# A hybrid decoder layer: sigmoids and gelu by hyperbolic tangents, and the convolution from an SBUF tile with carried columns

## The reference, cut to what matters

```python
lx = causal_depthwise_conv(lx, conv_w[i], conv_b[i])
r = sigmoid(gate_a); i = sigmoid(gate_x)
log_a = -LRU_C * r * softplus(-lam)
a = exp(log_a)
mult = sqrt(-expm1(2.0 * log_a))
bterm = mult * i * x
h[t] = a[t] * h[t-1] + bterm[t]
lru = h * gelu(lg)
mix = concatenate([rmsnorm(attn), rmsnorm(lru)])
x = x + mix @ w_out
```

## Time and profile before

| | us |
|---|---|
| median of 3 runs | 1447.66 |
| all three | 1447.93, 1447.66, 1443.44 |
| the profiled execution, its own time | 1447.09 |
| its span, slowest core (4) | 1445.4 |
| spans of the eight cores | 1414.2 to 1445.4 |
| mean granted TensorE clock, by core | 0.850 to 0.867 |

### The profile page before, as it was taken

How to read it: one execution, slowest core, us unless ns; L and a number is a source line. 1 busy time by engine, 2 the same in 40 slices (tenths; PEclk the granted TensorE clock), 3 DMA queues, 4 the chain that set the end, 5 groups by cost and what they waited for, 6 DMA issues and landing times.

```text
span 1445.4 us, 24745 instructions; the slowest of 8 cores (1414.2 to 1445.4 us)
## 1 busy us (share of the span) xinstructions
PE 1092.8 (76%) x7740; PEld 722.3 (50%) x7834; DVE 698.8 (48%) x1253; ACT 742.1 (51%) x1392; POOL 483.6 (33%) x576
## 2 busy tenths in 40 slices
PE   2535759988979897267697979988988797681892
PEld 1312225555555555156475757766766575550440
DVE  4879995977777864541121212211212121225853
ACT  4778897887877974012232423333333242224882
POOL 3212132332323333024242434433444243220663
PEclk9766777988978978559799989999999899895896
DMA  8999996963705932408999999999989989888422
GB/s 230 193 190 109 107 109 85 189 115 96 132 9 88 144 106 94 184 21 160 204 195 220 175 216 208 204 187 205 234 190 184 223 156 174 174 276 319 163 117 117
DMA packets 69775, 234.93 MB, mean 163 GB/s; under 512 B 23430, under 2 KB 30342, under 8 KB 51472
## 3 DMA queue, kind: packets, MB, share of 16 engines
q0 software_dynamic: 43984, 134.60, 57.1%
q1 hardware_dynamic: 25664, 98.75, 20.1%
HBM read 415.47 MB, written 101.71 MB: 358 GB/s over the span
## 4 chain that ended last, share of the span: by engine, by line
PE 44%; DMA 20%; issue 11%; DVE 9%; ACT 9%; POOL 4%; SPq 1%; another core or an unknown queue 0%; DVEq 0%; ACTq 0%; POOLq 0%
PE ps L1369 13%; DMA sb_R<-h2scr,sb_R 12%; PE ps L1341 7%; PE ps L967 4%; DMA sb_R<-wall,sb_R 3%; DMA sb_R<-w_pg 3%; PE ps L751 3%; PE ps L1324 2%; PE ps L1004 2%; PE ps L1512 2%; PE ps L841 2%; PE ps L903 1%; DMA sb_R<-xin 1%; PE ps L904 1%; PE ps L1245 1%
## 5 line engine op out<-in xcount | busy, mean ns | idle before, releaser
L1369 PE MATMUL ps<-sb_R 128*128 128x256 bf16 x3008 | 343.0, 275 | 5.3 <-DMA sb_R<-wall,sb_R 3.6
L1369 PEld LDWEIGHTS ps<-sb_R 128*128 128x128 bf16 x3008 | 296.0, 99 | 53.3 <-issue 6.7
L1351 POOL DMA_INDIRECT yscr<-sb_R x94 | 94.6, 1006 | 361.1 <-DVE sb_R L1348 344.9
L1374 DVE TENSOR_TENSOR sb_R<-sb_R,ps 128x512 bf16<-128x512 f32 x94 | 64.7, 688 | 296.9 <-PE ps L1369 268.8
L1327 ACT COPY sb_R<-ps 128x1024 bf16<-128x1024 bf16 x94 | 95.1, 1012 | 191.6 <-PE ps L1324 187.3
L1341 PE MATMUL ps<-sb_R 128*128 128x512 bf16 x706 | 171.2, 396 | 4.9 <-issue 2.1
L1348 DVE COPY sb_R<-ps 128x512 f32<-128x512 f32 x94 | 65.0, 692 | 222.5 <-PE ps L1341 140.2
L1373 ACT ACTIVATE sb_R<-ps 128x512 f32<-128x512 f32 x94 | 56.1, 597 | 224.8 <-PE ps L1369 224.7
L1295 POOL DMA_INDIRECT sb_R<-h2scr,sb_R x94 | 97.7, 1039 | 89.3 <-DVE sb_R L1254 60.9
L1341 PEld LDWEIGHTS ps<-sb_R 128*128 128x128 bf16 x752 | 74.5, 102 | 89.0 <-issue 19.8
L1324 PE MATMUL ps<-sb_id,sb_R 128*128 128x128 bf16 x752 | 58.1, 237 | 63.6 <-DMA sb_R<-h2scr,sb_R 63.1
(11 more groups left out here) (234 smaller groups left out, 2085.6 us busy)
## 6 DMA issues: line engine op xcount, KB each, us to landing
sb_R<-wall POOLq DMA_DIRECT2D x66, 1024.0 KB, 23.1
wbf<-wall POOLq DMA_DIRECT2D x30, 1024.0 KB, 46.0
sb_R<-wbf SPq DMA_DIRECT2D x30, 1024.0 KB, 13.2
sb_R<-xin SPq DMA_DIRECT2D x32, 512.0 KB, 20.3
sb_R<-yscr SPq DMA_DIRECT2D x16, 1024.0 KB, 8.1
xscr<-sb_R SPq DMA_DIRECT2D x16, 512.0 KB, 4.1
sb_R<-xscr SPq DMA_DIRECT2D x16, 512.0 KB, 13.4
out<-sb_R SPq DMA_DIRECT2D x16, 512.0 KB, 2.7
```

Of the source, the lines that this page charges most:

```text
L1351: return e.indirect_dma_start(y_d, bass.IndirectOffsetOnAxis(ap=didx[:, blk:blk + 1], axis=0), y.ap, None, bounds_check=breg(e, 2 * T_OWN ...
L1369: ins = e.matmul(pv[:, q * N:(q + 1) * N], lhsT=w_[:, c, f * P:(f + 1) * P], rhs=hT_[:, c, 0:N], start=(c == 0), stop=(c == 7))
L1374: S.op("dve", lambda e: e.tensor_tensor(hid[s % 2][:, fp * 2:fp * 2 + 2, 0:N], sgs[fp][:, 0:2 * N].rearrange("p (q t) -> p q t", q=2), pu. ...
```

## The change

Both sigmoids become 0.5 (1 + tanh(x/2)). One ACT pass makes each tanh; the halves go into the columns of constants (`der` 0 to 3) and into a bias of ln 0.5, so the decay is one Exp from the tanh and the two Ln and the Exp that inverted are gone. 1 + tanh is multiplied with the convolution by one DVE pass, which takes the place of the subtraction. The gelu has one tanh in the place of Exp, Ln, Exp; its factor of a half goes into the norm. The projection is copied by ACT from PSUM to an SBUF tile `lx` of 515 columns, whose first three POOL fills from `carry`; the four DVE passes read shifted pieces of it over the full 512 columns, and POOL saves the last three. There are two such tiles (`LX`), and `F5` shrinks from 12 to 10; `F10` stays at 14. The scheduler learns which functions share a table and ranks an ACT operation that needs another table 20 us lower.

```diff
+SWITCH = 20.0
+SETS = {AF.Exp: ("exp", "ln"), AF.Ln: ("ln",), AF.Tanh: ("exp",), AF.Silu: ("silu",), AF.Sigmoid: ("sig",), AF.Sin: ("sin",)}
...
-                    if e == "act" and o.table is not None and o.table != table:
-                        st += 1.4
-                    cand.append((st, -o.prio + ALPHA * o.idx, o.idx, o))
+                    sw = e == "act" and o.table is not None and table not in o.table
+                    cand.append((st, -o.prio + ALPHA * o.idx + (SWITCH if sw else 0.0), o.idx, o))
...
-            if o.eng == "act" and o.table is not None:
-                table = o.table
+            if o.eng == "act" and o.table is not None and table not in o.table:
+                table = o.table[0]
+                st += 1.3
...
-        F5 = R.pool(S, "f512", 512, 12)
+        F5 = R.pool(S, "f512", 512, 10)
+        LX = R.pool(S, "lx", 516, 2)
...
-            S.op("dve", lambda e: e.tensor_scalar(cv.ap, pl.ap, colp[:, cc, 3:4], colp[:, cc, 4:5], ALU.mult, ALU.add),
-                 reads=[pl, colp_b], writes=[cv])
+            lx = S.v(LX)
+            S.op("pool", lambda e: e.tensor_copy(lx[:, 0:3], carry[:, cc, 0:3]), reads=[carry_b[cc]], writes=[lx])
+            S.op("act", lambda e: e.copy(lx[:, 3:515], pl.ap), reads=[pl], writes=[lx])
+            S.op("dve", lambda e: e.tensor_scalar(cv.ap, lx[:, 3:515], colp[:, cc, 3:4], colp[:, cc, 4:5], ALU.mult, ALU.add), reads=[lx, colp_b], writes=[cv])
             for j in range(2, -1, -1):
-                sh = 3 - j
-                S.op("dve", lambda e, j=j, sh=sh: e.scalar_tensor_tensor(
-                    cv[:, sh:512], pl[:, 0:512 - sh], colp[:, cc, j:j + 1], cv[:, sh:512], ALU.mult, ALU.add),
-                    reads=[pl, colp_b, cv], writes=[cv])
-            if blk > 0:
-                for j in range(3):
-                    S.op("dve", lambda e, j=j: e.scalar_tensor_tensor(
-                        cv[:, 0:3 - j], carry[:, cc, j:3], colp[:, cc, j:j + 1], cv[:, 0:3 - j], ALU.mult, ALU.add),
-                        reads=[carry_b[cc], colp_b, cv], writes=[cv])
-            S.op("dve", lambda e: e.tensor_copy(carry[:, cc, 0:3], pl[:, 509:512]), reads=[pl], writes=[carry_b[cc]])
+                S.op("dve", lambda e, j=j: e.scalar_tensor_tensor(
+                    cv.ap, lx[:, j:j + 512], colp[:, cc, j:j + 1], cv.ap, ALU.mult, ALU.add),
+                    reads=[lx, colp_b, cv], writes=[cv])
+            S.op("pool", lambda e: e.tensor_copy(carry[:, cc, 0:3], lx[:, 512:515]), reads=[lx], writes=[carry_b[cc]])
...
-            S.op("act", lambda e: e.activation(t0.ap, pga.ap, A.Exp, scale=-1.0, bias=der[:, cc, 2:3]), reads=[pga, der_b], writes=[t0])
-            S.op("act", lambda e: e.activation(t4.ap, pgx.ap, A.Exp, scale=-1.0, bias=der[:, cc, 3:4]), reads=[pgx, der_b], writes=[t4])
-            S.op("act", lambda e: e.activation(t0.ap, t0.ap, A.Ln, bias=1.0), reads=[t0], writes=[t0])
-            S.op("act", lambda e: e.activation(t0.ap, t0.ap, A.Exp, scale=-1.0), reads=[t0], writes=[t0])
-            S.op("act", lambda e: e.activation(t2.ap, t0.ap, A.Exp, scale=der[:, cc, 0:1]), reads=[t0, der_b], writes=[t2])
-            S.op("act", lambda e: e.activation(t3.ap, t0.ap, A.Exp, scale=der[:, cc, 1:2]), reads=[t0, der_b], writes=[t3])
+            S.op("act", lambda e: e.activation(t0.ap, pga.ap, A.Tanh, scale=0.5, bias=der[:, cc, 2:3]), reads=[pga, der_b], writes=[t0])
+            S.op("act", lambda e: e.activation(t4.ap, pgx.ap, A.Tanh, scale=0.5, bias=der[:, cc, 3:4]), reads=[pgx, der_b], writes=[t4])
+            S.op("act", lambda e: e.activation(t3.ap, t0.ap, A.Exp, scale=der[:, cc, 1:2], bias=der[:, cc, 1:2]), reads=[t0, der_b], writes=[t3])
+            S.op("act", lambda e: e.activation(t2.ap, t0.ap, A.Exp, scale=der[:, cc, 0:1], bias=der[:, cc, 0:1]), reads=[t0, der_b], writes=[t2])
             S.op("act", lambda e: e.activation(t3.ap, t3.ap, A.Ln, scale=-1.0, bias=1.0), reads=[t3], writes=[t3])
-            S.op("act", lambda e: e.activation(t4.ap, t4.ap, A.Ln, bias=1.0), reads=[t4], writes=[t4])
-            S.op("dve", lambda e: e.scalar_tensor_tensor(t3.ap, t3.ap, 0.5, t4.ap, ALU.mult, ALU.subtract), reads=[t3, t4], writes=[t3])
-            S.op("act", lambda e: e.activation(t3.ap, t3.ap, A.Exp), reads=[t3], writes=[t3])
-            S.op("dve", lambda e: e.tensor_tensor(t3.ap, t3.ap, cv.ap, ALU.mult), reads=[t3, cv], writes=[t3])
+            S.op("act", lambda e: e.activation(t3.ap, t3.ap, A.Exp, scale=0.5, bias=lnh_ap), reads=[t3, eps_b], writes=[t3])
+            S.op("dve", lambda e: e.scalar_tensor_tensor(t4.ap, t4.ap, 1.0, cv.ap, ALU.add, ALU.mult), reads=[t4, cv], writes=[t4])
+            S.op("dve", lambda e: e.tensor_tensor(t3.ap, t3.ap, t4.ap, ALU.mult), reads=[t3, t4], writes=[t3])
...
-            S.op("act", lambda e: e.activation(t6.ap, t6.ap, A.Exp, scale=-GELU_C), reads=[t6], writes=[t6])
-            S.op("act", lambda e: e.activation(t6.ap, t6.ap, A.Ln, bias=1.0), reads=[t6], writes=[t6])
-            S.op("act", lambda e: e.activation(t6.ap, t6.ap, A.Exp, scale=-1.0), reads=[t6], writes=[t6])
+            S.op("act", lambda e: e.activation(t6.ap, t6.ap, A.Tanh, scale=0.5 * GELU_C), reads=[t6], writes=[t6])
```

More of the change, by code:

```diff
@@ L88, in activation @@
         self.c += 0.2 + fsize(in_) * 0.00083 + (0.2 if accum_out is not None else 0.0)
-        if func in (AF.Exp, AF.Ln):
-            self.table = "el"
-        elif func in (AF.Silu, AF.Sigmoid, AF.Sin):
-            self.table = func
+        if func in SETS:
+            self.table = SETS[func]
         return self
@@ L576 @@
 GELU_S = 0.044715 ** 0.5
+LN_HALF = -0.6931471805599453
 DEBUG_STOP = None
@@ L671, in build @@
         print("phase1 words", R.off, "of", RW)
-        mhalf = sb("mhalf", [P, 4]); mh_b = B("mh"); epst = sb("epst", [P, 1]); eps_ap = epst[:, 0:1]
-        S.op("dve", lambda e: e.memset(epst[:], EPS), writes=[eps_b])
+        mhalf = sb("mhalf", [P, 4]); mh_b = B("mh"); epst = sb("epst", [P, 2]); eps_ap = epst[:, 0:1]; lnh_ap = epst[:, 1:2]
+        S.op("dve", lambda e: e.memset(epst[:, 0:1], EPS), writes=[eps_b])
+        S.op("dve", lambda e: e.memset(epst[:, 1:2], LN_HALF), writes=[eps_b])
         S.op("dve", lambda e: e.memset(mhalf[:], -0.5), writes=[mh_b])
@@ L825, in lru_norm @@
             S.op("act", lambda e: e.activation(rbc.ap, pss.ap, AF.Ln, scale=1.0 / 512.0, bias=eps_ap), reads=[pss, eps_b], writes=[rbc])
-            S.op("act", lambda e: e.activation(rbc.ap, rbc.ap, AF.Exp, scale=-0.5), reads=[rbc], writes=[rbc])
+            S.op("act", lambda e: e.activation(rbc.ap, rbc.ap, AF.Exp, scale=-0.5, bias=lnh_ap), reads=[rbc, eps_b], writes=[rbc])
             for cc in range(4):
```

12 lines of the change are left out of this document (6 added, 6 removed).

## The result

The changed kernel takes 1486.8 us (median of 4 runs, 1484.2 to 1503.6) where the kernel before takes 1446.8 us (4 runs): ratio 1.027, 95% interval 1.024 to 1.030. It is slower, and the forecast of 1442 us with its range to 1460 missed it. In some executions, the one of 1503.6 us among them, one die runs at a lower granted clock and takes longer; the ratios leave these out. The profiled execution has a span of 1487.7 us on core 6.

What follows compares the result with a forecast made beforehand. No engine bounds the whole: VectorE sets the pace from 96 to 171 us, TensorE or chains of small steps from 235 to 577. Terms -1 - 3 - 3 + 2 = -5 us take 1447.1 to 1442 us; eight in ten within 1428 to 1460.

Steps and rivals of the forecast that it cites:

- The stage: First stage, to the last router tile near 577 us: holds all edited lines; its gain or loss passes on one to one.
- the term of -1: 96 to 171 us, blocks 0 to 3: ScalarE becomes the bound, 69 us at 93% filling is 74; -1 us, bounds -6 and +6.
- the term of -3 for blocks 5 to 7: 235 to 577 us: VectorE's work falls 12 us, ScalarE's by 0, TensorE waits less; -3 us, bounds -9 and +12.
- Up to 96 us: 0: Before w_out's load lands: nothing VectorE needs can be won, it only waits longer; 0 us.
- 96 to 171: ACT busier than DVE: Sign of being right: between 96 and 171 us ScalarE is busier than VectorE.
- ScalarE's sum: Whole of ScalarE: chunk passes -32, gelu -17, 35 added table loads +48; -1 us.
- VectorE's sum: Whole of VectorE: about 1.0 us saved per chunk over 32 chunks; -32 us, -24 with the dear scaling pass.
- +2: GpSimd's 64 copies of 3 columns as links in the chain: +2 us on the path, between 0 and +8.
- rival 2: Blocks 4 to 7 and 96 to 171: Ln and last Exp wait for a group, then a load; 1461 us, chance 0.18.
- Rival 3: Two convolution buffers, ten ring tiles and late GpSimd copies cost +6 to +10 at block changes; 1452 us, chance 0.05.
- Rival 4: ScalarE stands empty another 1.28 us behind each table load; 1471 us, chance 0.03.
- Rival 5: The table switches do not come, ScalarE is 48 us lighter; 1430 us, chance 0.02.

Runs made afterwards that it cites:

- e2: Changed kernel with w_out's scaling passes made to follow the last scan of block 3: last logits 589.0 us, 1.014 of the kernel before.
- e7: Changed kernel with w_out's scaling late and both carry copies on VectorE instead of GpSimd: last logits 584.2 us, 1.013 of the kernel before.
- e5: Changed kernel with Tanh emitted as Exp on the chip (output not the reference's) and w_out's scaling late: last logits 588.2 us, 1.017 of the kernel before.
- e9: Changed kernel, Tanh emitted as Exp (output not the reference's), w_out's scaling late, planned without a switch price: last logits 558.0 us, 0.991 of the kernel before.
- e6: Kernel before with the 512-column ring cut from 12 to 10 and one added dependence: last logits 578.1 us, 1.006 of the kernel before.
- e14: Changed kernel, w_out's scaling late, square root by a VectorE pass and a GpSimd power instead of Ln and Exp: 3958 us, 2.75 of the kernel before.
- e10: Changed kernel with real Tanh, w_out's scaling late, planned without a switch price, 73 table loads: last logits 607.8 us, 1.026 of the kernel before.

## Why the prediction was wrong, step by step

**The stage.** Right: 37.3 of the 40.2 us lie before the last router logits, and the rest of the program handed them on.

**The sum against the trace.** To the 16th scan 0 and -1 were forecast and +26 came; from there to the 20th, where the forecast has its 171 to 235, -3 and -1; from there to the last logits -3 and +12. The two steps that failed are the term of -1 (the work left behind the weights, and what stands still while VectorE waits) and the term of -3 for blocks 5 to 7 (an order that groups the switches was put at no cost but its loads).

**"Up to 96 us: 0."** The wait was foreseen (5.8 to over 10; it is 13.4 us, the load landing at 93.2), its consequence wasn't. With 3 scans ahead of the weights, as counted, I took the work behind them to be 60 to 63 us of VectorE and 69 of ScalarE at 93% filling, 74 us. By the stretch of the changed kernel from there to the 16th scan it took 101:

```profile
93.00:194.00 101.00, 51.83 (x212) 20.97 (x212) 86.00 (x129) 80.93 (x115) 36.67 (x51) 0.67 1.00 126
```

VectorE was busy 86 us, not 63, and ScalarE 81, not 69, at 85% and 80% filling; the kernel before had taken 76 us from the weights to its 16th scan. This term of -1 was +25. VectorE's largest groups in the stretch:

```profile
L763 DVE SCALAR_TENSOR_TENSOR sb_R<-sb_R,sb_colp 128x512 f32<-128x512 f32 x39 | 29.6, 767 | 1.0
L787 DVE TENSOR_TENSOR_SCAN sb_R<-sb_R 128x512 f32<-128x512 f32 x13 | 17.7, 1358 | 0.4 <-DVE sb_R L761 0.2
```

Two things were missed. More work lies in this stretch than I counted: these two groups alone are 47 us. Of the 39 products 27 belong to the sixteen chunks and 12 to the four of block 4, which the planner put ahead of the 16th scan together with the first keys and values; in the kernel before 6 products of block 4 stood there. And a pass that waits for a transfer stops everything behind it on its own queue and, through the cast and the carried columns, on two others. e2 showed what the place is worth: with the pass elsewhere all 26 us came back by the 16th scan.

**"96 to 171: ACT busier than DVE."** Wrong: the row answering to the earlier trace rows has VectorE 62.0 and ScalarE 59.2 of 75 us, neither setting the pace. From 235 to 577 us (second row) TensorE's granted clock is 0.88 against 0.86 before, so the clock is not what was lost there.

```profile
96.00:171.00 75.00, 37.97 (x145) 15.11 (x146) 62.03 (x91) 59.23 (x82) 28.38 (x40) 0.60 1.00 131
235.00:577.00 342.00, 297.14 (x2074) 174.93 (x2073) 253.28 (x470) 271.29 (x613) 121.07 (x170) 0.88 0.57 94
```

**ScalarE's sum.** 42 loads were forecast and 42 came, and none has a gap behind it of more than 0.013 us (347.80 + 1.28, next pass at 349.09). The two Exps with both a scale and a bias column last 0.81 us against 0.71 to 0.72 before, as the bound allowed. The total rose 7.4 instead of falling 1: a small miss.

**VectorE's sum.** -32 was forecast, -6.8 came. The corrections and the carry copy went as counted. What failed is above all the price of an SBUF pass. Groups of VectorE in the changed kernel up to 607 us, against the earlier trace rows:

```profile
L763 DVE SCALAR_TENSOR_TENSOR sb_R<-sb_R,sb_colp 128x512 f32<-128x512 f32 x96 | 74.5, 786 | 2.0 <-DVE sb_R L763 0.5
L761 DVE TENSOR_SCALAR sb_R<-sb_R,sb_colp 128x512 f32<-128x512 f32 x32 | 18.6, 586 | 5.5 <-ACT sb_R L760 5.0
```

The three products were to become 0.07 us shorter each and became 0.05 longer (741 to 786 ns), the scaling pass took 0.59 instead of 0.43 to 0.45. Single lines, before and after, show two causes for the products:

```profile
L759 DVE SCALAR_TENSOR_TENSOR sb_R<-ps,sb_colp,sb_R x96: 698/742/750, 37.7 to 468.5; 128x511 f32<-128x511 f32 x32, 128x510 f32<-128x510 f32 x32, 128x509 f32<-128x509 f32 x32
L763 DVE SCALAR_TENSOR_TENSOR sb_R<-sb_R,sb_colp x96: 697/746/1416, 37.2 to 488.1; 128x512 f32<-128x512 f32 x96
```

The median is the same from either source, 742 and 746 ns: the two-operand pass of 0.68 us, 0.60 apart, was the wrong row to price this pass by. And from SBUF some take up to twice as long, 0.83 us on average beside GpSimd's work; the last section has that. The products make up 11 of the 25 us missed, the scaling pass some 2; the rest is not accounted for here.

**GpSimd.** +20 us forecast on its engine, +43.5 came: the copies took 0.46 us each instead of 0.32, 29 us in all, and the gates' casts 9 more than before; on the path +2 was charged. e7 took its copies out of the chain and gained nothing that could be measured, so the +2 may stand.

**"235 to 577: -3."** Here failed the second large term. The loads were priced (half of 25 us), the order wasn't: "an Ln waits for a group" was written down in rival 2, but its price was taken from the loads alone. e5 against e9 gives the order 30 us with the same 7 loads in both. The count held against that rival, "only 6 of the 18 stand between the Exps of a block's attention", was of the wrong thing: what matters is how long one Ln stands ready behind Exps, 36 us at block 5.

**Which rival.** It was rival 2 in its mechanism and partly in its place, at 0.18 and 1461 us; what it lacked are the w_out term and the order's own price. It stood at 1461 us, just outside the range of 1428 to 1460, and even it is 26 us short. Rival 3's ring may be in the 8 us of e6, in the kernel before; in the changed one nothing of it was seen. Rival 4 is out by the rows. Rival 5, no switches, would have been 1430: e9, its order made for that case, ran at 0.991, 1434 on this scale, with the scaling late.

**The account** to the last logits, along the runs: the work without switches, in its own order, scaling late, -12 (558.0); the order that groups the switches +30 (588.2); the loads in that order +1 (589.0); w_out's scaling early +19 (607.7). Along another path the shares are others (loads 18 with the scaling early), since these waits cover each other; only the total of +37 is fixed. What stays open is why the convolution alone costs 27 us with the old gates.

## What to carry to other kernels

A scheduler's price for a table switch buys fewer loads with a longer chain: don't count only the switches in the new order, read how long the pass that needs the other table stands ready behind work that doesn't, and what hangs on it. The Trainium skill, page "ScalarE: Activation LUTs", section "Rules for kernel authors", says to group by table set and finish one set before switching; down to 45 loads that held here (607.8 to 580.2 us), and the last step, from 45 to 44, cost 9 us, in one pair of orders.

In engines that run in order, a pass that waits for a transfer belongs behind all work that doesn't need it. One extra dependence moved it here; whenever an edit shifts the order, look again at what stands behind each such pass.

Undo two suspects together before you add up their shares: 18 and 19 us made 20.

## What the runs showed of the hardware

**GpSimd's power of two tensors** takes 82.16 us at 128x512, some 160 ns a column, and 0.58 us at 128x1 and 0.84 at 128x2 in the kernel before (means; the 0.73 that the attempt's expectation names is a mean over both forms).

**VectorE and GpSimd slow each other in SBUF.** GpSimd's copy of three columns takes 0.18 us when VectorE stands (84.94) and 1.17 us beside VectorE's passes (98.85). VectorE's product takes 1.10 us (78.16) beside this row of GpSimd, and 0.75 (93.57) while GpSimd is idle:

```profile
77.64 1.08 POOL L767 CAST sb_R<-sb_R 128x512 bf16<-128x512 f32 x1
```

Over the changed kernel (core 6) 50 products without GpSimd beside them take 0.745 us on average and at most 0.753; the other 46 take 0.830. Read from PSUM, in the kernel before, 40 of the 96 run beside GpSimd and none takes more than 0.750.

GpSimd's casts went from 727 ns, with VectorE's convolution reading PSUM, to 1012, with it reading SBUF; with the carry copies off GpSimd (e7) they were 876. Over all kernels here (but e14) the means are 720 to 848 with PSUM and 834 to 1060 with SBUF, so the order counts as well. The Trainium skill, page "GPSIMD Engine Reference", section "Architecture", says that the two engines share one read and one write port; these rows agree in kind, and I had not priced it.

**A table load** takes 1.283 us in all 73 cases of e10, and the next pass starts at once. The Trainium skill, page "ScalarE: Activation LUTs", section "What ACT_TABLE_LOAD costs", adds a drain of 1380 ns; the traces don't show one, and the measurement decides.
